# Half of block 0's turns moved behind the last product at the five joints of a two-block transformer kernel

## What is computed

```python
h = h + head_group_mixer(rmsnorm(h, ...), ...)        # block 1: conv + retention
h = h + memory_cross_attention(rmsnorm(h, ...), ...)  # 4 heads, 256 memory tokens
h = h + sq_relu_mlp(rmsnorm(h, ...), up_w, down_w)
h = rmsnorm(h, norm_f_w)
x = x + hybrid_mixer(rms_norm(x, ...), ...)           # block 2: three branches, gated
x = x + memory_cross_attention_2(rms_norm(x, ...), ...)
x = x + swiglu(rms_norm(x, ...), ...)
return rms_norm(x, final_g)
```

## Time and profile before

| what | value |
|---|---|
| median of three runs | 913.3 us |
| the profiled execution | 913.01 us, its span 910.9 us |
| PE busy | 901.4 us (99%) |
| DVE busy | 661.6 us (73%) |
| ACT busy | 504.2 us (55%) |
| granted TensorE clock, mean | 0.999 |
| turns at the joints (L737) | 80 |

### The profile page before, as it was taken

One profiled execution on the slowest core, in us unless ns is written; L12 is line 12 of the kernel. 1 busy time (PEld: TensorE's weight loads), 2 busy tenths in 40 slices (PEclk: granted clock), 3 DMA queues, 4 the chain that ended last, 5 costly groups with the idle time before them and its releaser, 6 DMA issues.

```text
span 910.9 us, 12836 instructions
## 1 busy us (share of the span) xinstructions
PE 901.4 (99%) x5160; PEld 787.4 (86%) x5160; DVE 661.6 (73%) x920; ACT 504.2 (55%) x584; POOL 24.3 (3%) x69
## 2 busy tenths in 40 slices
PE   9999999999999999999999999999999999999997
PEld 8888998889888888888888988888899888888886
DVE  5799999987577666656967996646686676565665
ACT  6796435655555444445656757744464654544444
POOL 1600010000000000000000000000000000000000
PEclk9999999999999999999999999999999999999999
DMA  9746555454355666654755455455453456666551
GB/s 353 253 159 223 183 199 185 139 185 140 92 186 186 195 199 197 190 185 153 238 188 183 159 166 183 152 175 187 173 185 103 144 183 191 196 193 197 189 185 47
DMA packets 101280, 164.38 MB, mean 180 GB/s; under 512 B 2736, under 2 KB 71088, under 8 KB 101104
## 3 DMA queue, kind: packets, MB, share of 16 engines
q1 hardware_dynamic: 100528, 161.71, 54.2%
q0 software_dynamic: 560, 1.84, 0.7%
q10 hardware_dynamic: 144, 0.16, 0.1%
HBM read 162.65 MB, written 1.05 MB: 180 GB/s over the span
## 4 chain that ended last, share of the span: by engine, by line
PE 92%; DVE 5%; DMA 2%; ACT 1%; issue 1%; SPq 0%; DVEq 0%; ACTq 0%
PE ps L609 20%; PE ps L611 19%; PE ps L610 19%; PE ps L646 18%; PE ps L650 9%; DVE w_lo L1719 1%; DVE c_acc L1865 1%; DMA w_ring<-in_w_in 1%; PE ps L737 1%; DMA head_raw<-in_head 1%; PE ps L857 0%; ACT w_hi L1227 0%; PE ps L774 0%; DVE mem_l L1734 0%; PE ps L826 0%
## 5 line engine op out<-in xcount | busy, mean ns | idle before, releaser
L1719 DVE TENSOR_TENSOR w_lo<-w_ring,w_hi 128x2048 fp32r<-128x2048 f32 x146 | 333.4, 2288 | 114.2 <-ACT w_hi L1227 113.2
L1227 ACT ACTIVATE w_hi<-w_ring 128x2048 fp32r<-128x2048 f32 x146 | 278.6, 1911 | 88.3 <-DMA w_ring<-in_w_in 27.3
L646 PE MATMUL ps<-xx,w_hi 128*128 128x512 f32 x720 | 171.8, 391 | 0.3
L646 PEld LDWEIGHTS ps<-xx,w_hi 128*128 128x128 f32 x720 | 133.3, 188 | 27.4 <-issue 0.7
L609 PE MATMUL ps<-w_hi,xx 128*128 128x512 f32 x304 | 120.2, 395 | 0.0
L611 PE MATMUL ps<-w_hi,xx 128*128 128x512 f32 x304 | 118.6, 390 | 0.0
L610 PE MATMUL ps<-w_lo,xx 128*128 128x512 f32 x304 | 118.5, 390 | 0.0
L650 PEld LDWEIGHTS ps<-xx,w_lo 128*128 128x128 f32 x720 | 92.3, 191 | 3.5
L650 PE MATMUL ps<-xx,w_lo 128*128 128x256 f32 x720 | 93.4, 283 | 0.0
L609 PE MATMUL ps<-w_hi,ff_h 128*128 128x512 f32 (+1 forms) x218 | 84.7, 389 | 0.0
L610 PE MATMUL ps<-w_lo,ff_h 128*128 128x512 f32 (+1 forms) x218 | 84.6, 388 | 0.0
(11 more groups left out here) (339 smaller groups left out, 1335.9 us busy)
## 6 DMA issues: line engine op xcount, KB each, us to landing
w_ring<-in_w_in SPq DMA_DIRECT2D x34, 1024.0 KB, 5.1
w_ring<-in_mlp_up_w SPq DMA_DIRECT2D x16, 1024.0 KB, 5.6
w_ring<-in_mlp_down_w SPq DMA_DIRECT2D x16, 1024.0 KB, 4.9
w_ring<-in_w_gate_ffn SPq DMA_DIRECT2D x11, 1024.0 KB, 5.3
w_ring<-in_w_up_ffn SPq DMA_DIRECT2D x11, 1024.0 KB, 5.3
w_ring<-in_w_down_ffn SPq DMA_DIRECT2D x11, 1024.0 KB, 4.9
w_ring<-in_xkv_w SPq DMA_DIRECT2D x8, 1024.0 KB, 5.4
w_ring<-in_w_out SPq DMA_DIRECT2D x8, 1024.0 KB, 4.8
```

The costliest lines, as they stand in the source:

```text
L646: pe.matmul(feat(bank + b), wh[:, k, b * P:(b + 1) * P], xx[:, k, :, :].rearrange("p e t -> p (e t)"), start=k == 0, stop=False)
L1227: act.activation(w_hi[:, s, :], w_ring[:, s, :], ACT.Copy).then_inc(hi_done, 1)
L1719: dve.tensor_tensor(w_lo[:, s, :], w_ring[:, s, :], w_hi[:, s, :].bitcast(F32), ALU.subtract).then_inc(lo_done, 1)
```

## The change

At each joint only four of block 0's eight turns stay between the products of block 1. The other four go behind the last product, after two pieces of block 1; the two last pieces of block 1 come after them, in banks 7 and 3. The order stands in one list of six pieces (token block, bank, first feature block, end). ACT and DVE split in the order of that list, and the consumer's counts follow: k = 0 to 3 need 5 to 8 splits, k = 4 to 7 need 13 to 16. DVE now does four lo splits before the four adds of block 1, and twelve behind them.

```diff
-def raw_pieces(n, tb):
-
-
-    if tb == 0:
-        return [(0, 0, 4), (1, 4, 8)]
-    return [(bank, 2 * m, 2 * m + 2) for m, bank in enumerate((0, 2, 1, 3))]
-
-
-def pieces_before(n, tb):
-
-    return sum(len(raw_pieces(m, t)) for m in range(R_XA, n + 1) for t in range(2) if (m, t) < (n, tb))
+RAW_ORDER = [(0, 0, 0, 4), (1, 0, 0, 2), (1, 2, 2, 4), (0, 1, 4, 8), (1, 7, 4, 6), (1, 3, 6, 8)]
+
+
+def raw_done(n, k):
+
+    return 16 * (n - R_XA) + (5 if k < 4 else 9) + k
...
-            def raw_transpose(n, tb, upd=None):
-
-                first = {bank: k1 for bank, k0, k1 in raw_pieces(n, 0)}
-                for m, (bank, k0, k1) in enumerate(raw_pieces(n, tb)):
-                    if upd is not None:
-                        pe.wait_ge(h_updated, 6 * upd + 2 * tb + m + 1)
-                    if tb == 1 and bank in first:
-                        pe.wait_ge(raw_lo, 16 * (n - R_XA) + first[bank])
+            def raw_transpose(n, first, upd):
+
+                for m in range(1) if first else range(1, len(RAW_ORDER)):
+                    tb, bank, k0, k1 = RAW_ORDER[m]
+                    if tb == 0:
+                        pe.wait_ge(h_updated, 6 * upd + 1 + k0 // 4)
+                    else:
+                        pe.wait_ge(h_updated, 6 * upd + 3 + k0 // 2)
+                    if m == 1:
+                        pe.wait_ge(raw_lo, 16 * (n - R_XA) + 4)
                     for k in range(k0, k1):
                         mm = pe.transpose(ps[:, bank, (k - k0) * P:(k - k0 + 1) * P], h[:, tb, k * P:(k + 1) * P], ident[:, :])
                     mm.then_inc(raw_t, 1)
 
             def raw_ready(n):
 
-                return [lambda k, done=done: pe.wait_ge(done, 16 * (n - R_XA) + 9 + k) for done in (raw_hi, raw_lo)]
+                return [lambda k, done=done: pe.wait_ge(done, raw_done(n, k)) for done in (raw_hi, raw_lo)]
...
             form_b_rows(I_OUT1 + 2, 2 * OUT1_ORDER[2], x_t, (1,), False, False, kks=(0,))
-            raw_transpose(R_XA, 0, UPD[I_OUT1])
+            raw_transpose(R_XA, True, UPD[I_OUT1])
...
-            raw_transpose(R_XA, 1, UPD[I_OUT1])
-            x_attention(0, I_Q1, I_O1, raw_ready(R_XA), lambda: raw_transpose(R_MLP, 0, UPD[I_O1]))
-
-            raw_transpose(R_MLP, 1, UPD[I_O1])
+            raw_transpose(R_XA, False, UPD[I_OUT1])
+            x_attention(0, I_Q1, I_O1, raw_ready(R_XA), lambda: raw_transpose(R_MLP, True, UPD[I_O1]))
+
+            raw_transpose(R_MLP, False, UPD[I_O1])
...
-            def raw_split_hi(n, tb, which=range(4)):
-
-                for m, (bank, k0, k1) in enumerate(raw_pieces(n, tb)):
-                    if m not in which:
-                        continue
-                    act.wait_ge(raw_t, pieces_before(n, tb) + m + 1)
+            def raw_split_hi(n):
+
+                for m, (tb, bank, k0, k1) in enumerate(RAW_ORDER):
+                    act.wait_ge(raw_t, len(RAW_ORDER) * (n - R_XA) + m + 1)
...
-            def raw_split_lo(n, tb, which=range(4)):
-
-                t = slice(tb * P, (tb + 1) * P)
-                for m, (bank, k0, k1) in enumerate(raw_pieces(n, tb)):
-                    if m not in which:
+            def raw_split_lo(n, pieces):
+
+                done = 0
+                for m, (tb, bank, k0, k1) in enumerate(RAW_ORDER):
+                    done += k1 - k0
+                    if m not in pieces:
                         continue
-                    dve.wait_ge(raw_hi, 16 * (n - R_XA) + 8 * tb + k1)
+                    t = slice(tb * P, (tb + 1) * P)
+                    dve.wait_ge(raw_hi, 16 * (n - R_XA) + done)
...
                 for tb in range(TB):
                     update_block(tb)
-                    raw_split_lo(n, tb)
+                    raw_split_lo(n, range(1, len(RAW_ORDER)) if tb else (0,))
```

More of the change, by code:

```diff
@@ L1023, in mlp1 @@
                     form_b_rows(i + 2, 0, u_t, (1,), False, False, step=step, kks=(0,))
-                    raw_transpose(R_MIX2, 0, UPD[I_FF1])
+                    raw_transpose(R_MIX2, True, UPD[I_FF1])
                     form_b_rows(i + 2, 0, u_t, (1,), False, False, step=step, kks=(1,)).then_inc(slab_used, 1)
@@ L1036, in _ @@
             mlp1(G1 - 1, last=True)
-            raw_transpose(R_MIX2, 1, UPD[I_FF1])
+            raw_transpose(R_MIX2, False, UPD[I_FF1])
             form_a(I_SBQK, (0,), x_t, 256, 0, *raw_ready(R_MIX2))
@@ L1166, in _ @@
             form_b(I_OUT2, x_t, range(4), merged_ready,
[L1167 to L1171, removed]
+                   lambda: raw_transpose(R_XA2, True, UPD[I_OUT2]))
+            raw_transpose(R_XA2, False, UPD[I_OUT2])
+            x_attention(1, I_Q2, I_O2, raw_ready(R_XA2), lambda: raw_transpose(R_FF2, True, UPD[I_O2]))
+            raw_transpose(R_FF2, False, UPD[I_O2])
             def glu_in(i, gate_done=None, up_done=None, step=0, ready=(), last=False):
@@ L1271, in boundary @@
                 hi(nxt + 1)
-                raw_split_hi(n, 0)
-                raw_split_hi(n, 1)
+                raw_split_hi(n)
                 hi(nxt + 2)
@@ L1496, in _ @@
             act.wait_ge(gain_product, 1)
-            raw_split_hi(R_MIX2, 0)
-            raw_split_hi(R_MIX2, 1)
+            raw_split_hi(R_MIX2)
             for tb in range(TB):
@@ L2099, in _ @@
                 update_block(tb)
-                raw_split_lo(R_MIX2, tb)
+                raw_split_lo(R_MIX2, range(1, len(RAW_ORDER)) if tb else (0,))
             lo(I_SBQK + 1)
```

## The result

The changed kernel took 918.49 us (median of 6 runs, 917.95 to 918.73), the kernel before 913.67 us (6 runs, 912.95 to 915.75). The ratio is 1.0051, with a 95% interval of 1.0041 to 1.0061. The forecast was 917.4 us in a range of 914.3 to 919.9. The profiled execution took 918.25 us, with a span of 916.2 us.

A forecast was written before the change was run, and what follows sets the result against it. PE carries 92% of the waits, released at joints by the chain last product, hi split, lo split. Joint costs 1.05 + 0.30 + 0.76 + 1.05 + 0.98 = 4.1 us on 913.3 gave 917.4 us, range 914.3 to 919.9.

The forecast's parts named there:

- The hole behind the fourth turn: Behind the last product PE idles 0.32 us for DVE's add; the four moved turns fill it.
- The hole at the fifth k: In the first product, the fifth k's third matmul loads at 4.29 instead of 3.13; PE stands 1.16 us.
- The places downstream: Where PE next waits for DVE, whose queue behind the splits moves by 1.05 us at every joint.
- the scores at joints 1 and 4: First scores wait for DVE's `q_l`, with PE there before it: +1.05 us at each joint.
- the fourth slab at 3: At joint 3 this slab waits for DVE's sum of halves; reserve 0.29 us, cost +0.76 us.
- the third slab at 5: At joint 5 this slab's load waits for a DVE sum; cost +0.98 us.
- four turns fewer between the products: On PE at each joint, 4 x 0.124 = 0.50 us saved: the last product ends that much earlier.
- zero: Start of time counting at a joint: PE's load of the first turn behind the last product.
- At joint 2 the forecast: Only the direct wait at the fifth k counts, +0.30 us; `ff_l` downstream has 1.75 us reserve.
- Only the direct wait counts: Rival: PE loses 0.65 us three times and 0.30 twice, downstream reserves suffice; 2.55 us, 915.9; chance 0.14.
- The hole is filled and nothing opens behind it: Rival: no wait at the fifth k, every joint gains 0.50 us, 2.5 us in all; 910.8; chance 0.11.
- The clock falls: Rival: 1.2 GHz until the first slab is done, 5.7 us more per joint, 28 us; 945; chance 0.03.

The follow-up runs named there:

- second profile: The changed kernel run once more, unaltered, for another profile; 917.54 us (one run).
- Experiment 2: The kernel before plus one DVE instruction behind each joint's last lo split, whose result nobody reads; 917.87 us, ratio 1.0041.
- experiment 4: The change, with DVE's lo split of the next slab moved between block 0's adds and its lo splits; 916.38 us, ratio 1.0026.
- experiments 1 and 7: 1: kernel before, only DVE's lo-split order changed, 918.16 us. 7: the change, but six of block 0's turns between the products, two behind, 914.45 us.

## Why the prediction was right

**The mechanism** stood step by step. The hole behind the fourth turn closed and was worth nothing by itself: first third matmul at 1.70, predicted 1.71. The hole at the fifth k opened: 4.28, predicted 4.29. DVE waits 0.42 us for ACT ahead of the third piece (predicted 2.82 - 2.35 = 0.47), and reaches the slab at 4.93, predicted 4.93. The scores of joint 1 load 0.65 us behind the load before them (predicted "some 0.6 us or more"). The prediction did not have the 0.17 us that the fifth k's first matmul stands for its hi split; they cost nothing more, since the lo split comes later still.

**The places downstream** were right: the scores at joints 1 and 4, the fourth slab at 3, the third slab at 5, and, in the second profile, nothing at 2. At joint 5 PE stands first for the norm factor's `diag`, which the prediction did not name, and then for the third slab. Experiment 2 shows this with DVE's delay by itself, experiment 4 with it taken away.

**The sizes.** One term was mis-sized: four turns fewer between the products, put at 4 x 0.124 = 0.50 us. The stretch from the first turn there to zero is 192.72 - 188.14 = 4.58 us after, and was 192.87 - 187.90 = 4.97, so the term is 0.39. The eight took 0.99 us, the four that are left 188.70 - 188.14 = 0.56, and 0.99 / 8 is not the price of one: the stretch from the first turn's load to the second's holds the end of the product ahead. This shows when the loads on both sides are taken in, before:

```profile
187.67 0.19 PEld L611 LDWEIGHTS ps<-w_hi,xx 128*128 128x128 f32 x1
...
189.00 0.19 PEld L610 LDWEIGHTS ps<-w_lo,xx 128*128 128x128 f32 x1
```

and after:

```profile
187.92 0.19 PEld L606 LDWEIGHTS ps<-w_hi,xx 128*128 128x128 f32 x1
...
188.81 0.19 PEld L605 LDWEIGHTS ps<-w_lo,xx 128*128 128x128 f32 x1
```

Without turns these two loads, with one more between them, would stand two products apart, 2 x 0.23 = 0.46 us. They stand 1.33 us apart with eight turns and 0.89 with four, so the turns take 0.87 and 0.43, 0.11 us each. By the same mean the twelve behind zero were put at 1.50 us and took 1.42, which changes nothing further on. Four fewer give 0.44 us there, of which 0.39 are left at zero. That makes joints 1, 3, 4 and 5 dearer by 0.1 us, and they measured 0.05 to 0.10 above the forecast.

At joint 2 the forecast was met in the second profile, 0.30 us, and this was in part luck. The smaller term should have made it 0.41. What makes up for it is on PE's loads behind the wait, here in the first profile:

```profile
258.85 0.53 PEld L641 LDWEIGHTS ps<-xx,w_hi 128*128 128x128 f32 x3 [0.83 <-DVE xx L1740]
258.96 0.43 PEld L641 LDWEIGHTS ps<-xx,w_hi 128*128 128x128 f32 x2
```

The load behind the waiting one follows it by 0.11 us and not by the usual 0.23, so 0.12 us of the wait come back, for which the prediction had no term. The 0.5 us more at joint 2 in the first profile go with a slab's landing time, which the prediction had no term for either and the repeat does not show.

**The rivals.** *Only the direct wait counts* (915.9) is refuted by experiment 2, where there is no direct wait and 3.9 us are lost, and by experiments 1 and 7. *The hole is filled and nothing opens behind it* (910.8) needed splits faster than 0.26 us apart; the twelve splits of ACT take 3.21 us, (3.21 - 0.38) / 11 = 0.257 each. *The clock falls* (945) did not happen either. The stretch of the twelve turns and the wait, 192.72 to 197.35 (length; busy time of PE, PEld, DVE, ACT, POOL with counts; granted clock):

```profile
192.72:197.35 4.63, 3.97 (x31) 3.51 (x29) 3.66 (x13) 3.99 (x13) 0.00 (x0) 1.00 1.08 363
```

The granted clock stayed at 1.00, the 2.4 GHz level, through twelve turns in a row and more than 1 us of standing. By the rule of the Trainium skill that spoke for that rival (TensorE: Matmul & The Clock Gate, Part 4: PE-mode transpose) the full clock would not engage for transposes; no row here bears that out.

## What to carry to other kernels

An idle slot on the bound engine is worth filling only if the work put there is not followed by a chain through other engines that the next product waits for: cost the chain of every moved piece to its last link, here turn, hi split, lo split, in the order of each engine's own list. A piece that one engine takes later is late in the queues of all that follow it, and whatever stands behind it there is late too; where such an engine is busy 95% of a stretch, as DVE is here behind joint 1, the delay comes out at its next meeting point in full, less that point's reserve. Two waits behind one cause are not to be added where the engine that stands at the first reaches the second later by it: the longer delay is what it pays. Price a removed instruction from how a whole run of them changes, not from a mean that takes in a part of its neighbour.

## What was not expected of the hardware

A turn takes 0.11 us in runs of four, eight and twelve alike. From the first load to the load behind them four took 0.56 us, eight 0.99 and twelve 194.14 - 192.72 = 1.42 us, 0.108 us for each more. The 0.13 us over that look like a price for having a run at all, but they belong to the product ahead of it, as the loads on both sides show. And the same slab, in two executions of the same kernel, kept ACT waiting 2.31 and 0.98 us; in these two executions that went with PE standing 0.5 us or not at all.
